# Query strips of the even layer, expert panels parted by contraction, and sample projections without a fold

## The chip, the cores and the metric

The kernel runs on one NeuronCore of one Trainium2 chip. The metric is the device time of one launch in microseconds (us), from the first to the last instruction and what lies around them. The core has five engines with instruction queues of their own: TensorE (PE; its weight loads are shown apart as PEld), VectorE (DVE), ScalarE (ACT), GpSimd (POOL) and SyncE (SP), which here only issues DMAs. They wait for each other by semaphores. PE's results go to PSUM, eight banks of 128 partitions by 512 fp32 numbers, and are copied or consumed from there by DVE and ACT. All weights stream from HBM through 16 DMA engines that the queues share.

## What is computed

One inference step of a two-layer decoder trunk on 256 prompt tokens (one sequence) and 32 sample tokens (8 sequences of 4), with a model width of 1024, all in fp32. Layer 0 ("even") is gated linear attention with 4 heads, in chunks of 16 tokens, beside a pooling mixer; layer 1 ("odd") is retention. Each is followed by a mixture of 64 experts with the 8 best per token and a shared expert, and then by a gate. Cut to what matters here:

```python
def step(S, inp):                       # even layer, one chunk of 16 (prompt) or 4 (sample) tokens
    qc, kc, vc, ac = inp
    b = jnp.cumsum(ac, axis=1)
    q_in = qc * jnp.exp(b)
    k_in = kc * jnp.exp(-b)
    o_inter = jnp.einsum('bchk,bhkv->bchv', q_in, S)      # queries times the carried state
    att = jnp.where(causal, jnp.einsum('bthk,bshk->bhts', q_in, k_in), 0.0)
    o_intra = jnp.einsum('bhts,bshv->bthv', att, vc)
    ...
    return S_new, o_inter + o_intra
...
mixed = jnp.concatenate([o_a, pooled], axis=-1)
return mixed @ w_out, ...                                  # out projection
...
x = layer_norm(ALPHA * x + h, ...)
h = jax.nn.silu(xt @ wg) * (xt @ wu)                       # one expert; its result is (h @ wd) * gate
x = layer_norm(ALPHA * x + f, ...)
gate = jax.nn.sigmoid(x @ w_ple_gate[i])                   # gates of each token
x = x + gate * (p[i] @ w_ple_proj[i])
```

## The kernel before

The order of the work is written out by hand, engine by engine; one function per engine and layer part, and semaphores between them. PSUM banks are dealt out by `plan_groups`, which walks the names of `group_order` and gives each the next bank in turn; PE's `begin(name)` waits until the bank's last user has freed it, and `end(...)` marks it full. `CH` names three chunks of tokens: 0 and 1 are the prompt's two halves of 128, 2 the 32 sample tokens.

**Queries times states (`even_pe`, L901 and L907).** The states that the 16 chunks carry lie in `SS` (head pair f, chunk i), those of the sample's 8 sequences in `gs0`. For each chunk but the first, the state (128 by 128) is the stationary operand and 32 query columns (two heads by 16 tokens) move; for each sequence 8 columns move. The results go straight into the banks `oT` (features by tokens) and `oTs`; behind them the pooling matrices follow (L912), then masked attention times values is added in the same banks (L919, L924). ACT squares and copies `oT`, PE sums the squares (L931), and the out projection follows (L1158, L1162, L1116).

**Sample rows of the out projection and of the gates (`tok`, L1105, and `fold`, L1124).** The contraction has 8 parts; part c goes with all 512 columns into the strip of 32 partitions number c % 4, so that four partial sums lie in four strips. ACT copies them to SBUF (`keep_strips`), and a matmul with a stacked identity adds them up (`fold`); DVE (`residual`, L2262) or ACT (`gate_half`) takes the sum of 32 rows. Each wide matrix has two column halves n, so this runs twice for the out projection of layer 0 and twice for the gates of each layer.

**Experts.** They go in pairs: `gate_up` (L1252), `turn_hidden` (L1259), `down` (L1266) and the sums of the pair before (L1228, L1224). A pair's weights are three panels of 2 MB in a ring of six slots: panel k = 0 and 1 each hold gate and up matrix of one expert of the pair, panel 2 both down matrices. `gate_up` waits for both of its panels before its first matmul. SP refills a slot when the bank that its panel's last matmul fills is marked; the first three pairs of loads stand before a loop, the rest in `two_pairs` (L768 to L781). One pair (`HOME`, the seventeenth in order) has its weights in SBUF outside the ring.

The names that the steps touch: `QI` (scaled queries), `QS` and `QSS` (new), `parts` and `Steps.empty`, which takes four strips with 128 columns each out of a bank, one instruction per strip.

Of the kernel before, what the change touches and what calls it, by code (L numbers as in the profile page):

```python
# [31 lines left out]
P = 128  # L32
# [14 lines left out]
H = 4  # L47
# [65 lines left out]
def constants():  # L113
# [17 lines left out]
            np.tile(inv.reshape(-1), (P, 1))]  # L131
# [50 lines left out]
def group_order():  # L182
# [6 lines left out]
    def out(tag, chunks=range(3)):  # L189
        g.extend((tag, j, n) for j in chunks for n in range(2))  # L190
        if 2 in chunks and tag[:2] in ("ou", "pg"):
            at = g.index((tag, 2, 1)) + 1
            g[at:at] = [(tag, "fold", n) for n in range(2)]

    for l in range(DEPTH):
        xt(f"xTa{l}", ORD[2:] if l else ORD)
        if l % 2 == 0:
# [59 lines left out]
        g.extend((f"pg{l}", "fold", n) for n in range(2))  # L257
        g.extend((f"pg{l}", 1, n) for n in range(2))
        if l + 1 < DEPTH:
# [56 lines left out]
def trunk(nc, A, O, C):  # L316
# [17 lines left out]
    with ExitStack() as ctx:  # L334
# [64 lines left out]
        invc = ce.take(64)  # L399

# [14 lines left out]
        QI = a.take(4 * T).rearrange("p (f k t) -> p f k t", f=2, k=2)  # L415
# [14 lines left out]
        AT = XTb[:, 4 * T:8 * T].rearrange("p (h t) -> p h t", h=4)  # L430

# [88 lines left out]

        def strip_sums(name):

            at = STATE if name[0] == "out0" else SIDE
            o = 0 if name[0] == "out0" else D
            return at[:, o + 512 * name[2]:o + 512 * name[2] + 512]
# [110 lines left out]
        def _(sp):  # L636
# [41 lines left out]
            for l in range(DEPTH):  # L678
# [57 lines left out]

                for pr in range(2):
                    for k in range(3):
# [25 lines left out]
                        expert_panel(n0 + 3 * pr + k, 2 * pr, k)  # L764
# [3 lines left out]
                def two_pairs(it, late):  # L768
                    for u in range(1 if isinstance(it, int) else 2):
# [7 lines left out]
                with sp.Fori(1, HOME // 2 + 1) as it:  # L777
# [3 lines left out]
                two_pairs(PAIRS // 2 - 1, 1)  # L781
# [27 lines left out]
        def even_pe(pe, st, begin, end, feat, tok):  # L809
# [75 lines left out]
            for h in range(H):  # L885
                ps = begin(("att", h))
                for j, (o, r) in enumerate(CH):
                    last = pe.matmul(ps[0:r, o:o + r], KI[:, h // 2, o:o + r], QI[:, h // 2, h % 2, o:o + r],
                                     start=True, stop=True)
                end(last, ("att", h))  # L890
# [5 lines left out]
            outs = []  # L896
# [6 lines left out]
            out4 = begin(("oTs",))[:, 0:H * TS].rearrange("p (h t) -> p h t", h=H)  # L903
            for f in range(2):
                for i in range(NSEQ):
                    c = DSEQ * i
                    pe.matmul(out4[:, 2 * f:2 * f + 2, c:c + DSEQ], gs0[:, f, i, :], QI[:, f, :, SEQ + c:SEQ + c + DSEQ],  # L907
                              start=(f == 0 and i == 0), stop=False, skip_group_check=True)
# [6 lines left out]
            for f in range(2):  # L915
                for k in range(2):
                    h = 2 * f + k
                    for j in range(2):
                        last = pe.matmul(outs[f][:, k, P * j:P * j + P], V[:, j, P * h:P * h + P],  # L919
                                         AT[:, h, P * j:P * j + P], start=False, stop=(k == 1 and j == 1),  # L920
                                         skip_group_check=True)
                end(last, ("oT", f))
            for h in range(H):
                last = pe.matmul(out4[:, h, :], V[0:TS, 2, P * h:P * h + P], AT[0:TS, h, SEQ:T],  # L924
                                 start=False, stop=(h == H - 1), skip_group_check=True)
# [7 lines left out]
        def odd_pe(pe, st, begin, end, feat, tok, fold, transpose_x):  # L933
# [122 lines left out]
        def _(pe):  # L1056
# [40 lines left out]
            def tok(name, lhs, rhs, r, n, w=512):  # L1097
# [3 lines left out]
                if r == TS and n >= 8 and name[0] not in ("v", "out1", "oute1"):  # L1101
# [17 lines left out]
            def fold(tag):  # L1119

                for n in range(2):
                    emptied(pe, (tag, 2, n))
                    ps = begin((tag, "fold", n))
                    end(pe.matmul(ps[0:TS, :], fold4, strip_sums((tag, 2, n)), start=True, stop=True), (tag, "fold", n))  # L1124

            pe.wait_ge(sem("ident_in"), 16)
            pe.wait_ge(sem("ones_set"), 1)
            for l in range(DEPTH):
# [9 lines left out]
                else:  # L1138
                    odd_pe(pe, st, begin, end, feat, tok, fold, transpose_x)
                if l % 2 == 0:  # L1140
# [23 lines left out]
                    fold(f"out{l}")  # L1164
# [90 lines left out]

                def turn_hidden(u, ps):
# [48 lines left out]
                def two_pairs(it, late=False):  # L1305

                    for u in range(2):
# [9 lines left out]
                        else:  # L1317
# [1201 lines left out]
```

## Time and profile before

| | |
|---|---|
| time, median of 3 runs (range) | 1671.39 us (1671.09 to 1671.58) |
| the profiled execution: its own time, its span | 1670.99 us, 1669.2 us |
| busy share of the span: PE, DVE, ACT, POOL | 95%, 32%, 20%, 9% |
| bytes from HBM, to HBM | 526.15 MB, 23.87 MB |
| mean granted TensorE clock | 0.983 |

The span runs from the first instruction to the last one; the rest of the execution's own time lies around it. The profile gives each instruction's start and length, what ended the idle time in front of it, and the TensorE clock that was granted (1.00 is 2.4 GHz, 0.50 is 1.2 GHz). In an instruction's line "ps<-arena 128*128 128x32" the first pair is the stationary operand, the second the result. Each fp32 matmul of the program stands as two instructions in the trace. The stages, in us from the span's start: the even layer to 172, routing to 210, experts of layer 0 to 699, gates to 748, the odd layer to about 1091, routing to 1129, experts of layer 1 to 1616, gates to the end.

### The profile page before, as it was taken

The page shows a single profiled execution, that of the slowest core. Times are in us where ns is not written, and L with a number is a line of the kernel's source. Part 1 is how long each engine was busy: PE and PEld are TensorE (multiplying, and loading weights), DVE is VectorE, ACT ScalarE, POOL GpSimd, SP SyncE. Part 2 cuts the span into 40 slices and gives each one's busy share as a digit, 9 for nine tenths or more (in the row PEclk, how much of TensorE's full clock was granted, in tenths as well). Part 3 has the DMA queues.
Part 4 walks back from the last instruction along what each step waited for, and adds up shares of the span by engine and source line. Part 5 has one row for each costly group of instructions (what it writes and reads, how often), then busy time and mean ns, then how long its engine had stood idle before and what let it go on. Part 6 is the DMA issues. An engine that isn't in the chain of part 4 may idle for free.

```text
span 1669.2 us, 21844 instructions
## 1 busy us (share of the span) xinstructions
PE 1587.6 (95%) x7954; PEld 799.2 (48%) x7954; DVE 539.7 (32%) x1322; ACT 341.4 (20%) x693; POOL 144.6 (9%) x221
## 2 busy tenths in 40 slices
PE   8999899999999999999999999989999999999998
PEld 5784544334344433446665755554443434443343
DVE  2145722222222222261434245372222222222225
ACT  2102122121122221231222222012212112221122
POOL 0330100000000000000011111010000000000000
PEclk9969999999999999999999999989999999999999
DMA  9623779999989999955385586577999998999970
GB/s 299 245 82 133 277 313 419 421 421 420 420 348 421 420 420 420 388 200 188 134 269 195 196 279 235 202 310 306 421 421 421 420 419 362 420 421 419 421 291 29
DMA packets 119271, 536.09 MB, mean 321 GB/s; under 512 B 17849, under 2 KB 29369, under 8 KB 69408
## 3 DMA queue, kind: packets, MB, share of 16 engines
q1 hardware_dynamic: 95975, 470.35, 70.5%
q0 software_dynamic: 21360, 61.64, 10.2%
q10 hardware_dynamic: 1872, 3.22, 0.6%
q8 instruction: 44, 0.72, 0.2%
q14 instruction: 20, 0.16, 0.0%
HBM read 526.15 MB, written 23.87 MB: 330 GB/s over the span
## 4 chain that ended last, share of the span: by engine, by line
PE 81%; DMA 11%; DVE 3%; issue 2%; ACT 1%; SPq 1%; POOL 0%; ACTq 0%; DVEq 0%
PE ps L1252 23%; PE ps L1116 12%; PE ps L1094 12%; DMA weights<-in_w_exp_up 11%; PE ps L1266 10%; PE ps L1228 5%; PE ps L1245 3%; PE ps L1224 2%; PE ps L1259 1%; PE ps L1010 1%; PE ps L1105 1%; PE ps L1286 1%; PE ps L988 1%; PE ps L901 1%; PE ps L1001 1%
## 5 line engine op out<-in xcount | busy, mean ns | idle before, releaser
L1252 PE MATMUL ps<-weights,x_feat 128*64 128x512 f32 x1984 | 437.8, 593 | 36.8 <-DMA weights<-in_w_exp_up 18.5
L1252 PEld LDWEIGHTS ps<-weights,x_feat 128*64 128x64 f32 x1984 | 147.1, 137 | 320.9 <-issue 318.2
L1266 PE MATMUL ps<-weights,arena 128*64 128x512 f32 x992 | 226.5, 598 | 0.9 <-ACT arena L1450 0.9
L1094 PE MATMUL ps<-x_feat,weights 128*128 128x288 f32 x832 | 210.2, 411 | 1.1 <-ACT x_feat L1450 1.1
L1094 PEld LDWEIGHTS ps<-x_feat,weights 128*128 128x128 f32 x832 | 159.9, 194 | 45.1 <-issue 3.8
L2104 DVE CAST split<-state 128x1024 fp32r<-128x1024 f32 (+1 forms) x66 | 44.7, 678 | 324.9 <-ACT state L1450 324.9
L2101 DVE SCALAR_TENSOR_TENSOR arena<-arena,ps 128x256 f32<-128x256 f32 x64 | 30.7, 480 | 365.3 <-ACT arena L1679 365.3
L2423 POOL DMA_INDIRECT arena<-x_rows,arena x64 | 63.6, 993 | 891.0 <-DVE arena L2094 845.9
L1450 ACT ACTIVATE state<-ps 128x512 f32<-128x512 f32 x132 | 78.8, 597 | 268.5 <-PE ps L1266 261.1
L1116 PE MATMUL ps<-weights,x_feat 128*128 128x512 f32 x288 | 126.7, 594 | 3.0 <-ACT x_feat L1476 3.0
L1266 PEld LDWEIGHTS ps<-weights,arena 128*64 128x64 f32 x992 | 65.7, 136 | 132.3 <-issue 130.9
L1679 ACT ACTIVATE arena<-ps 128x256 f32<-128x256 f32 x64 | 24.5, 383 | 444.6 <-PE ps L1252 444.6
L1228 PE MATMUL ps<-split,token_rows 128*128 128x512 f32 x256 | 111.8, 437 | 1.6 <-DVE y_low L2107 1.6
L1450 ACT ACTIVATE arena<-ps 128x256 f32<-128x256 f32 (+7 forms) x150 | 59.0, 405 | 222.4 <-PE ps L1116 84.5
L1228 PE MATMUL ps<-y_low,token_rows 128*128 128x512 f32 x256 | 100.8, 394 | 0.0
L1116 PEld LDWEIGHTS ps<-weights,x_feat 128*128 128x128 f32 x288 | 54.1, 190 | 69.8 <-issue 64.5
L1245 PEld LDWEIGHTS ps<-const,arena 128*128 128x128 f32 x512 | 62.3, 194 | 51.1 <-issue 51.1
L1116 PE MATMUL ps<-weights,arena 128*128 128x512 f32 x192 | 84.3, 592 | 0.0
L1450 ACT ACTIVATE x_feat<-ps 128x512 f32<-128x512 f32 x137 | 74.0, 588 | 49.8 <-PE ps L1245 45.9
L2107 DVE TENSOR_TENSOR y_low<-state,split 128x1024 fp32r<-128x1024 f32 (+1 forms) x66 | 78.7, 1193 | 2.3
L1245 PE MATMUL ps<-const,arena 128*128 128x128 f32 x512 | 74.4, 288 | 0.0
L1116 PEld LDWEIGHTS ps<-weights,arena 128*128 128x128 f32 x192 | 36.1, 190 | 41.6 <-issue 41.1
(289 smaller groups left out, 1280.8 us busy)
## 6 DMA issues: line engine op xcount, KB each, us to landing
weights<-in_w_exp_gate SPq DMA_DIRECT2D x124, 1024.0 KB, 14.8
weights<-in_w_exp_up SPq DMA_DIRECT2D x124, 1024.0 KB, 18.8
weights<-in_w_exp_down SPq DMA_DIRECT2D x124, 1024.0 KB, 16.9
weights<-in_w_in_c SPq DMA_DIRECT2D x24, 1024.0 KB, 8.1
arena<-in_state_ret POOLq DMA_DIRECT2D x20, 512.0 KB, 5.5
out_ret_sample<-arena POOLq DMA_DIRECT2D x20, 512.0 KB, 6.5
weights<-in_w_in_a SPq DMA_DIRECT2D x8, 1024.0 KB, 10.9
weights<-in_w_ple_gate SPq DMA_DIRECT2D x8, 1024.0 KB, 17.8
```

The costliest lines, as they stand in the source:

```text
L1094: last = pe.matmul(ps[:, 0:T], lhs(c), XT[:, c, :], start=(c == 0), stop=(c == n - 1))
L1116: last = pe.matmul(ps[0:r, 0:w], lhs(c), rhs(c), start=(c == 0), stop=(c == n - 1))
L1224: last = pe.matmul(PS[TS * q:TS * q + TS, 7, 0:256], TOK[u][:, SEQ:T].bitcast(F32), YF[:, 256 * q:256 * q + 256], start=False, stop=stop, ...
L1228: last = pe.matmul(bank((f"sum{l}", j, n)), TOK[u][:, P * j:P * j + P], y[:, 512 * n:512 * n + 512], start=False, stop=stop and y is YLO, ...
L1245: last = pe.transpose(ps[:, c * P:c * P + P], xc[:, 4 * q + c, :], ident)
L1252: last = pe.matmul(ps[64 * s:64 * s + 64, :], XGT[u][:, c, 64 * s:64 * s + 64], rhs, start=(c == 0), stop=(c == KC - 1))
L1266: last = pe.matmul(ps[64 * s:64 * s + 64, :], HT[u][:, c, 64 * s:64 * s + 64], wd[s][:, c, 512 * n:512 * n + 512], start=(c == 0), stop=(c ...
L1450: return act.activation(dst, src, ACT.Copy, **k)
L2101: return STT(HH[u], HS[u], META[u][:, 0:1], PS[:, 0, DE:2 * DE], ALU.mult, ALU.mult)
L2104: return dve.tensor_copy(YHI[:, c], YF[:, c])
L2107: return TT(YLO[:, c], YF[:, c], YHI[:, c].bitcast(F32), ALU.subtract)
L2423: pool.indirect_dma_start(XG[u], None, xd, bass.IndirectOffsetOnAxis(ap=GI[u], axis=0), bounds_check=last_row, oob_is_err=False).then_inc( ...
```

## The change

Three parts, in one change.

1. **Query strips.** The two operands change places: 32 query columns of a chunk are stationary, the state's 128 columns move, and the result (32 tokens-by-heads rows) goes to strip i % 4 of the new banks `qS` and `qSs`. `QI` gets a layout with those 32 columns side by side. For the sample, one stationary operand holds the queries of four sequences, so that a strip has rows of other sequences too. ACT copies the three banks to SBUF (`QS`; for `QSS` with a mask per partition, `own_strip`), and PE turns them with 8 matmuls against the identity and 4 against the stacked one, adding them to `oT` and `oTs`. The first chunk takes part now, with a state that POOL sets to zero. The pooling matmuls stand before the new banks' use.
2. **Panels parted by contraction.** For the first and the last pair of each layer's ring, panel 0 holds parts 0 to 3 of the contraction of all four gate and up matrices, and panel 1 parts 4 to 7. `gate_up_halves` waits for each panel apart. After the first half of the very first pair it raises `half_consumed`, and SP refills that panel's slot upon it instead of upon the end of the whole gate-and-up. SP's second pair of pairs is written out ahead of its loop.
3. **No fold.** The sample rows of the out projection (layer 0) and of the gates (both layers) run with the branch that was there for other products: each strip takes 128 of the 512 columns over the whole contraction, 32 matmuls instead of 8. `fold` and `keep_strips` are gone, and the reader takes four pieces of 32 by 128.

```diff
@@ group_order
+            g.extend((("qS", 0), ("qS", 1), ("qSs",)))
+            g.extend(("pool", f) for f in range(4))
             g.extend((("oT", 0), ("oT", 1), ("oTs",)))
-            g.extend(("pool", f) for f in range(4))
...
@@ trunk
+        QS = [STATE[:, 512 * f:512 * f + 512] for f in range(2)]
+        QSS = keys[:, 0:512]
...
@@ SP
+                def contraction_panel(num, e0, k):
+
+                    s = slot_full[num % SLOTS]
+                    dst = wp(num).rearrange("p (s m x) -> p s m x", s=2, m=2)
+                    for m, w in enumerate((A["w_exp_gate"], A["w_exp_up"])):
+                        src = w[l, e0:e0 + 2].rearrange("e (p c) n -> p e (c n)", c=KC)
+                        sp.dma_start(dst[:, :, m, :], src[:, :, 1024 * k:1024 * k + 1024]).then_inc(s, 16)
...
+                            elif isinstance(it, int) and it == 1 and u + k == 0:
+                                sp.wait_ge(sem("half_consumed"), l + 1)
                             else:
                                 sp.wait_ge(bank_full[0], base[0] + 2 * (u + late) - 3 + 4 * it)
-                            expert_panel(n0 + 3 * u + k, 4 * it + 2 * u, k)
...
@@ even_pe
             for f in range(2):
-                out2 = begin(("oT", f)).rearrange("p (k t) -> p k t", k=2)
-                outs.append(out2)
-                for i in range(1, NCA):
-                    pe.matmul(out2[:, :, CA * i:CA * i + CA], SS[:, f, i, :], QI[:, f, :, CA * i:CA * i + CA],
-                              start=(i == 1), stop=False, skip_group_check=True)
...
+                ps = begin(("qS", f))
+                for i in range(NCA):
+                    q, g = i % 4, i // 4
+                    last = pe.matmul(ps[TS * q:TS * q + TS, P * g:P * g + P], QI[:, f, i].rearrange("p k c -> p (k c)"), SS[:, f, i, :],
+                                     start=(g == 0), stop=(g == 3), skip_group_check=True)
+                end(last, ("qS", f))
...
+                emptied(pe, ("qS", f))
+                for g in range(4):
+                    tokens_of = out2[:, :, 64 * g:64 * g + 64].rearrange("p k (i c) -> p i k c", c=CA)
+                    last = pe.matmul(tokens_of, QS[f][:, P * g:P * g + P], ident, start=False, stop=(g == 3),
+                                     skip_group_check=True)
...
+            emptied(pe, ("qSs",))
+            for f in range(2):
+                for g in range(2):
+                    last = pe.matmul(out4[:, 2 * f:2 * f + 2, CA * g:CA * g + CA], QSS[:, P * (2 * f + g):P * (2 * f + g) + P],
+                                     fold_all[:, 0:TS], start=False, stop=(f == 1 and g == 1), skip_group_check=True)
...
@@ tok
-                if r == TS and n >= 8 and name[0] not in ("v", "out1", "oute1"):
+                if name[0] == "vstrips":
...
@@ PE, experts
+                def gate_up_halves(u, ring, it, ps):
+                    for k in range(2):
+                        n = ring + k
+                        pe.wait_ge(slot_full[n % SLOTS], 32 * (n // SLOTS + 1) + 32 * it)
+                        w = wp(n).rearrange("p (s m c n) -> p s m c n", s=2, m=2, c=4)
+                        for c in range(4):
+                            for s in range(2):
+                                last = pe.matmul(ps[64 * s:64 * s + 64, :], XGT[u][:, 4 * k + c, 64 * s:64 * s + 64],
+                                                 w[:, s, :, c, :], start=(k == 0 and c == 0), stop=(k == 1 and c == 3))
+                        if it == 0 and k == 0:
+                            last.then_inc(sem("half_consumed"), 1)
+                    return last
...
@@ ACT, even layer
+                    for f in range(2):
+                        full(act, ("qS", f))
+                        st.free(copy(QS[f], bank(("qS", f))), ("qS", f))
+                    full(act, ("qSs",))
+                    act.wait_ge(sem("even_table"), 16)
+                    st.free(copy(QSS, bank(("qSs",)), scale=own_strip), ("qSs",))
...
@@ DVE residual
-                name, r = (f"out{l}", "fold" if j == 2 else j, n), CH[j][1]
+                name, r = (f"out{l}", j, n), CH[j][1]
...
-                st.free(STT(x, x, ALPHA, bank(name)[0:r, :], ALU.mult, ALU.add), name)
+                st.empty(name, r, lambda ps, c: STT(x[:, c], x[:, c], ALPHA, ps[0:r, :], ALU.mult, ALU.add))
```

PE's order in the even layer from the last state updates on, as it was; `ps` is PSUM, `arena` the region that holds states, queries and values, `ln_rows` holds `gs0`, and an `x` behind a shape counts matmuls (not trace instructions).

```order
L855 MATMUL ps<-arena,side 64x128 x32
L901 MATMUL ps<-arena 128x2x16 x30
L907 MATMUL ps<-arena,ln_rows 128x2x4 x16
L912 MATMUL ps<-arena 128x288 x4
L919 MATMUL ps<-x_feat,arena 128x128 x8
L924 MATMUL ps<-x_feat,arena 128x32 x4
L931 MATMUL ps<-x_feat,small 128x512 x2
```

The same place now; the lines are those of the changed kernel, `state` is `QS`, and L938 and L948 are the matmuls against the identities.

```order
L866 MATMUL ps<-arena,side 64x128 x32
L912 MATMUL ps<-arena 32x128 x32
L919 MATMUL ps<-ln_rows,arena 32x128 x16
L925 MATMUL ps<-arena 128x288 x4
L933 MATMUL ps<-x_feat,arena 128x128 x4
L938 MATMUL ps<-const,state 128x4x2x16 x4
L933 MATMUL ps<-x_feat,arena 128x128 x4
L938 MATMUL ps<-const,state 128x4x2x16 x4
L943 MATMUL ps<-x_feat,arena 128x32 x4
L948 MATMUL ps<-const,arena 128x2x16 x4
L955 MATMUL ps<-x_feat,small 128x512 x2
```

The 46 products of 128 rows have become 48 of 32 rows, and 12 matmuls have come in between attention and the squares.

SP's queue where the ring's first refill is issued, before (gate and up matrices of the second expert and both down matrices follow in the same way).

```order
L766 TENSOR_LOAD small [waits flag_ready]
L766 ISA x2
L777 UNCONDITIONAL_BRANCH
L777 ISA
L734 ISA [waits bank_full_0]
L734 DMA weights<-in_w_exp_gate 128x2048
L734 DMA weights<-in_w_exp_up 128x2048
```

And now.

```order
L771 TENSOR_LOAD small [waits flag_ready]
L771 ISA x2
L728 DMA weights<-in_w_exp_gate 128x2048 [waits half_consumed]
L728 DMA weights<-in_w_exp_up 128x2048
L728 DMA weights<-in_w_exp_gate 128x2048 [waits bank_full_0]
L728 DMA weights<-in_w_exp_up 128x2048
L728 DMA weights<-in_w_exp_down 128x2048 [waits bank_full_1]
```

Nothing has moved past anything there; the first refill stands ahead of the loop now and waits for another semaphore.

DVE's order around the sample rows of layer 0's out projection, before.

```order
L2276 TENSOR_SCALAR x_tok<-x_tok,small 128x1024
L2294 TENSOR_SCALAR x_feat<-ps,small 128x128 x4
L2262 SCALAR_TENSOR_TENSOR x_tok<-x_tok,ps 32x512 x2
L2269 BN_STATS small<-x_tok 32x6 x2
L2271 BN_AGGR small<-small 32x2
```

And now.

```order
L2312 TENSOR_SCALAR x_tok<-x_tok,small 128x1024
L2330 TENSOR_SCALAR x_feat<-ps,small 128x128 x4
L2298 SCALAR_TENSOR_TENSOR x_tok<-x_tok,ps 32x128 x8
L2305 BN_STATS small<-x_tok 32x6 x2
L2307 BN_AGGR small<-small 32x2
```

Two instructions of 512 columns have become eight of 128, in the same place.

## Rows read from the trace of the kernel before

**Rows 1.** Waits of PE over the whole span: us in total, times, longest us.

```profile
PE ps L1252 <- DMA weights<-in_w_exp_up: 18.5, 16, 1.6
PE ps L1252 <- issue: 16.0, 12, 1.6
```

**Rows 2.** Timeline of PE, even layer's end: start, us, instruction, idle before it.

```profile
97.43 6.33 PE L855 MATMUL ps<-arena,side 32*64 32x128 f32 x64 [2.97 <-DVE side L1806]
103.69 13.01 PE L901 MATMUL ps<-arena 128*128 128x32 f32 x60
116.51 6.97 PE L907 MATMUL ps<-arena,ln_rows 128*128 128x8 f32 x32
123.33 4.19 PE L912 MATMUL ps<-arena 128*128 128x288 f32 x8
127.31 2.75 PE L919 MATMUL ps<-x_feat,arena 128*128 128x128 f32 x16
130.00 1.07 PE L924 MATMUL ps<-x_feat,arena 32*128 32x32 f32 x8
```

**Rows 3.** Windows of PE there: us, busy (instructions), granted clock, DMA share, GB/s.

```profile
94.00:97.00 3.00, 0.46 (x5) 1.00 0.22 67
99.00:128.00 29.00, 29.00 (x150) 0.50 0.18 41
129.00:131.00 2.00, 2.00 (x18) 1.00 0.00 0
```

**Rows 4.** Timeline of ACT, even layer's end.

```profile
129.21 0.60 ACT L1541 ACTIVATE x_feat<-ps 128x512 f32<-128x512 f32 x1 [41.37 <-PE ps L919]
```

**Rows 5.** Timeline, other places: 288 columns at full clock; 32-row products, layer 1.

```profile
79.47 7.93 PE L1094 MATMUL ps<-x_feat,weights 128*128 128x288 f32 x32
...
1028.33 1.96 PE L1111 MATMUL ps<-weights,arena 128*32 128x128 f32 x64
...
1030.35 1.22 DVE L1971 SCALAR_TENSOR_TENSOR x_tok<-x_tok,ps 32x128 f32<-32x128 f32 x4 [1.23 <-PE ps L1111]
```

**Rows 6.** Windows in layer 0's expert stage, columns as in rows 3.

```profile
210.00:217.00 7.00, 6.95 (x32) 1.00 0.01 2
217.00:219.00 2.00, 1.53 (x13) 1.00 0.60 66
...
320.00:440.00 120.00, 109.40 (x573) 1.00 1.01 420
460.00:480.00 20.00, 20.00 (x110) 1.00 0.68 273
```

**Rows 7.** Timeline of SP's queue, layer 0: first refills of the ring.

```profile
217.32 0.35 SPq L734 DMA_DIRECT2D weights<-in_w_exp_gate  x1
...
230.71 0.33 SPq L734 DMA_DIRECT2D weights<-in_w_exp_gate  x1
```

**Rows 8.** Timeline of PE: first and last pair's gate-and-up, layers 0 and 1.

```profile
210.05 7.09 PE L1252 MATMUL ps<-weights,x_feat 128*64 128x512 f32 x32 [1.13 <-ACT x_feat L1450]
681.64 7.09 PE L1252 MATMUL ps<-weights,x_feat 128*64 128x512 f32 x32 [1.62 <-issue]
1598.93 7.09 PE L1252 MATMUL ps<-weights,x_feat 128*64 128x512 f32 x32 [1.49 <-issue]
```

**Rows 9.** Timeline, layer 0's out projection: sample rows, copies, fold, residual.

```profile
161.49 3.64 PE L1105 MATMUL ps<-weights,arena 128*32 128x512 f32 x32
164.26 1.36 DVE L2294 TENSOR_SCALAR x_feat<-ps,small 128x128 f32<-128x128 f32 x4
166.31 0.68 DVE L2262 SCALAR_TENSOR_TENSOR x_tok<-x_tok,ps 32x512 f32<-32x512 f32 x1 [0.69 <-PE ps L1124]
```

**Rows 10.** Timeline, layer 0's gates: fold, last feature turn, last logits.

```profile
729.33 1.90 PE L1124 MATMUL ps<-side,const 128*32 128x512 f32 x4
729.44 1.36 DVE L2294 TENSOR_SCALAR x_feat<-ps,small 128x128 f32<-128x128 f32 x4 [7.50 <-PE ps L1082]
731.17 14.00 PE L1116 MATMUL ps<-weights,x_feat 128*128 128x512 f32 x32
```

More of the change, by code:

```diff
@@ L399, in trunk @@
         invc = ce.take(64)
+        own_strip = ce.take(1)
         gate_ops = a.take(8 * RANK + 256 + T)
@@ L763, in _, with two_pairs @@
                         wait_slot(n0 + 3 * pr + k)
-                        expert_panel(n0 + 3 * pr + k, 2 * pr, k)
+                        if pr == 0 and k < 2:
+                            contraction_panel(k + n0, 0, k)
+                        else:
+                            expert_panel(n0 + 3 * pr + k, 2 * pr, k)
                 sp.wait_ge(sem("flag_ready"), l + 1)
                 go = sp.value_load(flagi[0:1, 0:1], min_val=0, max_val=1)
-                def two_pairs(it, late):
-                    for u in range(1 if isinstance(it, int) else 2):
+                def two_pairs(it, late, pairs=2):
+                    for u in range(pairs):
                         for k in range(3):
@@ L887, in even_pe @@
                 for j, (o, r) in enumerate(CH):
-                    last = pe.matmul(ps[0:r, o:o + r], KI[:, h // 2, o:o + r], QI[:, h // 2, h % 2, o:o + r],
-                                     start=True, stop=True)
+                    last = pe.matmul(ps[0:r, o:o + r], KI[:, h // 2, o:o + r],
+                                     QI[:, h // 2, o // CA:(o + r) // CA, h % 2, :], start=True, stop=True)
                 end(last, ("att", h))
@@ L915, in even_pe @@
             for f in range(2):
+                out2 = begin(("oT", f)).rearrange("p (k t) -> p k t", k=2)
                 for k in range(2):
@@ L931, in even_pe, with odd_pe @@
                 end(pe.matmul(ps, onesA, SQE[:, :, o:o + r], start=True, stop=True), ("ms", j))
-        def odd_pe(pe, st, begin, end, feat, tok, fold, transpose_x):
+        def odd_pe(pe, st, begin, end, feat, tok, transpose_x):
             for kind, h, i in odd_schedule():
@@ L1117, in tok @@
                 end(last, name)
[L1119 to L1124, printed above, removed]
             pe.wait_ge(sem("ident_in"), 16)
@@ L1138, in _ @@
                 else:
-                    odd_pe(pe, st, begin, end, feat, tok, fold, transpose_x)
+                    odd_pe(pe, st, begin, end, feat, tok, transpose_x)
                 if l % 2 == 0:
@@ L1316, in two_pairs @@
                             pe.wait_ge(sem("home_in"), 96 * (l + 1))
-                        else:
+                        elif not (first or last):
                             for n in range(ring, ring + 2):
@@ L1320, in two_pairs @@
                         pe.wait_ge(bank_free[0], base[0] + uses(0, pr, 0))
-                        gate_up(u, HOME_UP if home else [wp(ring), wp(ring + 1)], PS[:, 0, :]).then_inc(bank_full[0], 1)
+                        if first or last:
+                            gate_up_halves(u, ring, it, PS[:, 0, :]).then_inc(bank_full[0], 1)
+                        else:
+                            gate_up(u, HOME_UP if home else [wp(ring), wp(ring + 1)], PS[:, 0, :]).then_inc(bank_full[0], 1)
                         pe.wait_ge(bank_free[1], base[1] + uses(1, pr, 0))
@@ L1462, in norm_root @@
                 st.tell(act.activation(rstd[:, j:j + 1], bnag[:, 2 * j + 1:2 * j + 2], ACT.Sqrt, bias=eps), sem("std", l, k))
-            def keep_strips(tag):
-                for n in range(2):
-                    full(act, (tag, 2, n))
-                    st.free(copy(strip_sums((tag, 2, n)), bank((tag, 2, n))), (tag, 2, n))
             def x_affine(tag, l, k, chunks):
@@ L1723, in gate_half @@
                     r = CH[j][1]
-                    name = (f"pg{l}", "fold" if j == 2 else j, n)
+                    name = (f"pg{l}", j, n)
                     full(act, name)
@@ L1727, in gate_half @@
                         act.wait_ge(sem("gated", l), 2 * i + n - 1)
-                    st.free(act.activation(SG[n][0:r, :], bank(name)[0:r, :], ACT.Sigmoid), name)
+                    st.empty(name, r, lambda ps, c: act.activation(SG[n][0:r, c], ps[0:r, :], ACT.Sigmoid))
                 def gate(i):
@@ L1792, in even_dve @@
                         dve.wait_ge(sem("queries_zeroed"), 1)
-                    st.run(STT(QI[0:64, f, 0, :], ps[0:64], DKA ** -0.5, EB[0:64, f, :], ALU.mult, ALU.mult))
-                    st.free(STT(QI[64:128, f, 1, :], ps[64:128], DKA ** -0.5, EB[64:128, f, :], ALU.mult, ALU.mult), ("qk", f))
+                    for k in range(2):
+                        rows = slice(64 * k, 64 * k + 64)
+                        ins = STT(QI[rows, f, :, k, :], ps[rows].rearrange("p (i c) -> p i c", c=CA), DKA ** -0.5,
+                                  EB[rows, f, :].rearrange("p (i c) -> p i c", c=CA), ALU.mult, ALU.mult)
+                        if k:
+                            st.free(ins, ("qk", f))
+                        else:
+                            st.run(ins)
                 else:
@@ L2225, in gate @@
                 for n in range(2):
-                    emptied(dve, (f"pg{l}", "fold" if j == 2 else j, n))
+                    emptied(dve, (f"pg{l}", j, n))
                     cols = slice(512 * n, 512 * n + 512)
@@ L2328, in even_pool @@
             store(O["pool_sample"][0, :, 0:PBUF - DSEQ, :], A["state_pool"][0, :, DSEQ:PBUF, :], s)
+            st.run(pool.memset(SS[:, :, 0, :], 0.0))
+            st.after
             st.tell(pool.memset(QI, 0.0), sem("queries_zeroed"))
```

46 lines of the change are left out of this document (20 added, 26 removed), and 2 rows, old and new, of the table FIXED_BANKS.

## The prediction

> **What bounds the kernel now.** TensorE. I read the page first for its busy shares (PE 95% by the table above), then the list of PE's waits. Only one kind of wait comes back often: L1252, the gate-and-up of an expert pair, for its weights, 28 times with 34.5 us in all [rows 1]. That is the most that earlier loads can give. The second kind of loss is not idle time: in the windows [rows 3] PE is busy for the whole of 99 to 128 us, but at half the clock (0.50, which is 1.2 of 2.4 GHz). So in two places of the program two different things are to be counted: durations at the granted clock where PE is full, and arrival times where it waits for DMA.
>
> **Even layer's end, what goes.** PE waits 2.97 us for DVE at 94.46, does the state updates L855, and from 103.69 on runs without a gap to 131.07 [rows 2]. The parts: L901 13.01 us for 60 instructions and L907 6.97 for 32 (both 0.217 each, though one moves 32 columns and the other 8), L912 4.19 for 8, L919 2.75 for 16, L924 1.07 for 8. The whole is 131.07 - 103.69 = 27.38 us. All stands before the squares, the out projection and the routing, which follow from its end, so that each us saved here is one of the total, if nothing else becomes late. What could: ACT had been idle for 41.37 us at that point [rows 4], so the three new copies (0.60 us each by the same row's form) find it free and lie behind PE's pooling products.
>
> **What comes.** 48 strip products are 96 instructions. Layer 1 has products of the same shape, 128 by 32 stationary, 128 columns moving, four strips in turn: L1111, 64 in 1.96 us, 0.0306 each at full clock [rows 5]. At half clock I double that: 0.061, 5.9 us for 96. The other bound is L855, in place and at half clock, 6.33/64 = 0.099 each [rows 2], 9.5 us; but it has two strips of 64 columns instead of four of 32, so I take L1111's price. The pooling L925 costs 2.0 us at full clock (L1094, also 288 columns, 7.93/32 = 0.248 each [rows 5]) and 4.2 at half. Then come 16 instructions of attention times values, 16 turns, 8 of the sample and 8 more turns: 48. L924 at full clock has 1.07/8 = 0.134 each, and I take it for all: 6.4 us at full clock.
>
> So the clock decides. In [rows 2, 3] it is at 1.00 up to 97, at 0.50 from 99 to 128, and at 1.00 again from 129; the products with 288 columns had begun at 123.33, 5.6 us before, and before them narrow ones had run for 20 us without raising it. The strips move 128 columns, four of them side by side. I take it that the clock rises 5.6 us after the first of them: 5.9 + 2.0 + 6.4 = 14.3 us, **13.1 us gained**. If only the pooling products raise it, they take 4.2, and 1.4 us more at 0.268 do 5 of the 48; the rest is 43 x 0.134 = 5.8. The sum is then 5.9 + 4.2 + 1.4 + 5.8 = 17.3, 10.1 gained. A clock that never falls would take at most 3 us off the strips: 16 gained.
>
> Here a rule stands against the size of this gain. The Trainium skill, "TensorE: Matmul & The Clock Gate", section "LDWEIGHTS (loading the stationary operand)", gives the time of a weight load as its columns over 1.2, in ns, whatever the rows: 107 ns for 128 columns, 27 for 32. If loads set the pace at that price, 92 x 0.107 = 9.8 us would go and 96 x 0.027 + 24 x 0.107 = 5.2 come, an estimate of 4.6 us from that page. The trace disagrees on the size here: 0.217 per instruction at granted clock 0.50 [rows 2, 3].
>
> **First pair of a layer.** All loads of the ring's first six slots are done before its first matmul: the DMA share is 0.01 in 210 to 217 [rows 6], which is the first gate-and-up, 7.09 us from 210.05 [rows 8]. The first refill goes out at 217.32 [rows 7], in the two us behind it hardly anything moves (66 GB/s), and later the engines are full: 420 GB/s in 320 to 440, where PE is busy for 109.40 of 120 us [rows 6]. There DMA sets the pace, so bytes that flow earlier come off PE's waits. `half_consumed` comes after half of the 7.09 us, at about 213.85 by count of instructions: 217.32 - 213.85 = 3.44 us earlier. Panel 0 alone is freed then; panel 1 still waits for 217.3, but 2.1 MB at 420 GB/s keep the engines in work for 5.0 us, longer than the 3.44. The next place where the queue could run dry is the refill issued at 230.71 [rows 7]: three panels of 2.1 MB and 0.5 MB gathered take 16.2 us at that rate, from 215.9 (213.85 and the two us behind an issue) to 232.1, while what is issued at 230.71 flows by 232.7. Up to 0.6 us are lost there. I take **3.1 us**, between 2.8 and 3.44. It is kept: after the home pair the share falls to 0.68 for 20 us [rows 6], since the ring is full, so that DMA then follows PE. Layer 1 runs the same instructions: 3.1 again.
>
> **Last pair.** PE waits 1.62 us at 681.64 and 1.49 at 1598.93 for panel 1 [rows 8]. Panel 0 lands one panel, 5.0 us, earlier; its half takes 3.5 us of PE, more than the wait, so both waits go: **3.1 us**. The down panel follows panel 1 by 5.0 us, to some 686.6. PE asks for it once gate-and-up is through, 681.64 - 1.62 + 7.09 = 687.1, and hidden rows are turned; the slack is small, and a loss of up to 1 us stays in the range.
>
> **No fold.** In layer 0 the last in the chain is DVE: L2294 at 164.26 until 165.62, then the residual, 0.68 per half [rows 9], begun at 166.31 after the fold. Four pieces of 32 by 128 take 1.22 in L1971 [rows 5], so eight 2.44 instead of 1.36, but they begin when L2294 ends: 165.62 + 2.44 = 168.1. The two halves of now end at 166.31 + 1.36 = 167.7 at the earliest, later if the fold's second half keeps the second one waiting. So 0 to 0.4 are lost; I take **0.2 us**. PE's strips stay about as they are (3.64 now [rows 9], 128 x 0.0306 = 3.9 by L1111). At the gates the fold of 1.90 us ends at 731.2, when L1116 begins, but the last feature turn of that chunk ends on DVE at 729.44 + 1.36 = 730.80 [rows 10]: that is what L1116 then waits for, and 0.4 us gained pays the strips' 0.2 to 0.3. I count nothing for both layers, plus or minus 0.5.
>
> **Sum.** 13.1 + 6.2 + 3.1 - 0.2 = 22.2 us off the profiled execution's 1671.0 gives 1648.8. That execution lies 0.4 under the median of the three runs, so I say **1649 us**.
>
> **The rivals.** No change can be told from none within 0.2%, 3.3 us, and a mechanism on the far side has to eat 22 us first.
> - *The clock rises only with the pooling* (0.16): 3.0 us less, 1651.8. For it: 20 us of busy PE with narrow products did not raise it, and neither did L855 with its 128 columns.
> - *Strips at L855's price and a late clock* (0.10): 3.6 us more on top, 1655.4. For it: the same place and clock. Against: the strips of L1111.
> - *The refill's gain is swallowed* (0.12): if panels of 4 KB rows load slower, or the queue runs dry at 230.71 for longer, the 6.2 us are lost: 1655.0. Against: the full engines in [rows 6].
> - *The last pair's wait moves to its second half or to the down panel* (0.04): 1652.
> - *The turns give it back* (0.02): stationary operands of 128 columns set the pace to the end of the stage, at L901's 0.217 for each of the 48: 5.9 + 4.2 + 10.4 = 20.5, 6.9 gained, 1655.2. Against: L924, whose operand has 128 columns too, took 0.134. By the page cited above, with its 4.6 us, it would be 1657.3.
> - *Slower* (0.03): the clock stays at 0.50 behind the strips, through squares and out projection to 165.1. The 34 us of PE work there then take 68, 1649 + 34 = 1683. It decides when half clock lasts about 22 us longer than to 131. For it: PE has a new place to wait, for ACT's copies before the turns. Against: 4 us of pooling and attention products stand in between, and copies of 0.60 us are done by then.
> - *More* (0.02): the clock doesn't fall, 1646.
>
> The forecast has 0.51 and its own range, 1647 to 1650.5. The cases of 1651.8 to 1655.4 belong in the range, and below it the bounds of the refill and of the clock: 1645 to 1656. Faster by over 0.2%: all but the slower case and what I can't name, 0.95; same 0.02; slower 0.03.
>
> **What would show it.** The strips L912 and L919 together at 5.9 us or 9.5; the granted clock at 1.00 from about 109 or from about 115; `oTs` done at about 118 instead of 131. ACT's copies without a wait of PE at L938. SP's first refill 3.4 us after gate-and-up begins, and waits of L1268 in layer 0 some 3 us less before the home pair; no wait ahead of the last gate-and-up, and none inside it. Eight residuals of 0.31 in layer 0; L1140 following DVE's last turn in the gates. The forecast is wrong if DMA turns out to have had slack elsewhere, or if the stage from 103.7 on is not followed by what depends on it alone.

## The result, and the profile after

The changed kernel takes 1653.49 us (median of 4 runs, 1651.97 to 1655.55) against 1671.24 before: a ratio of 0.9895, 95% interval 0.9878 to 0.9912, so 17.7 us less where 22.2 were forecast. The profiled execution took 1652.17 us with a span of 1650.4, 18.8 less than before's.

What answers to [rows 2]: PE's timeline at the even layer's end, after.

```profile
96.97 6.50 PE L866 MATMUL ps<-arena,side 32*64 32x128 f32 x64 [2.98 <-DVE side L1842]
103.41 3.64 PE L912 MATMUL ps<-arena 128*32 128x128 f32 x64
106.82 1.56 PE L919 MATMUL ps<-ln_rows,arena 128*32 128x128 f32 x32
108.32 2.21 PE L925 MATMUL ps<-arena 128*128 128x288 f32 x8
110.36 1.05 PE L933 MATMUL ps<-x_feat,arena 128*128 128x128 f32 x8
111.25 1.06 PE L938 MATMUL ps<-const,state 128*128 128x128 f32 x8
...
115.03 1.08 PE L948 MATMUL ps<-const,arena 128*128 128x32 f32 x8
115.94 2.18 PE L955 MATMUL ps<-x_feat,small 128*128 128x512 f32 x6
```

In a MATMUL line the second pair is the moving operand, partitions by columns, and not the result: a strip `128*32 128x128` moves 128 columns and yields 32 rows. From the first strip to the squares it is 115.94 - 103.41 = 12.53 us, where it was 131.00 - 103.69 = 27.31. No wait stands ahead of L938, so ACT's copies are hidden. The windows of PE there (columns as in [rows 3]):

```profile
106.00:107.00 1.00, 1.00 (x24) 0.50 0.00 0
107.00:108.00 1.00, 1.00 (x29) 0.56 0.00 0
108.00:109.00 1.00, 1.00 (x19) 1.00 0.02 8
```

The clock is back at some 107.9, 4.5 us after the first strip and before any pooling product has begun. In [rows 3] it was at 0.50 until 128.

SP's first refills, which answer to [rows 7], and the windows of the expert stages, which answer to [rows 6]:

```profile
199.02 0.33 SPq L728 DMA_DIRECT2D weights<-in_w_exp_gate  x1
...
202.45 0.33 SPq L728 DMA_DIRECT2D weights<-in_w_exp_gate  x1
...
215.84 0.33 SPq L728 DMA_DIRECT2D weights<-in_w_exp_gate  x1
```

```profile
209.00:215.00 6.00, 6.00 (x30) 1.00 1.03 427
215.00:221.00 6.00, 6.00 (x39) 1.00 0.88 328
221.00:227.00 6.00, 6.00 (x30) 1.00 1.02 422
...
1131.00:1137.00 6.00, 6.00 (x39) 1.00 0.89 299
```

The first refill goes out 3.43 us ahead of the second. But behind the issue at 215.84, the one that [rows 7] has at 230.71, the rate dips to 328 GB/s, in layer 1 to 299: at 422 GB/s, six such us lack 6 x 94 / 422 = 1.3 and 6 x 123 / 422 = 1.7 us of transfer.

PE's waits, to be held against [rows 1], and PE's timeline at the last pairs' first products and at the end of layer 1's experts (the first line stands at the edge of a shorter stretch and counts 10 of the 32 instructions):

```profile
PE ps L1268 <- DMA weights<-in_w_exp_up: 14.6, 13, 1.6
PE ps L1268 <- issue: 13.0, 10, 1.6
...
PE ps L1140 <- issue: 2.7, 1, 2.7
```

```profile
662.24 2.31 PE L1279 MATMUL ps<-weights,x_feat 128*64 128x512 f32 x10
...
1577.35 7.04 PE L1279 MATMUL ps<-weights,x_feat 128*64 128x512 f32 x32
...
1594.57 0.40 PE L1244 MATMUL ps<-y_low,token_rows 128*128 128x512 f32 x1
1597.71 7.13 PE L1140 MATMUL ps<-weights,arena 128*128 128x512 f32 x16 [2.75 <-issue]
```

The waits for weights are 27.6 us instead of 34.5, and neither last pair (L1279) waits. New is 2.75 us ahead of layer 1's first projection. Held against before, the same places of PE's program come earlier by:

| place | us earlier |
|---|---|
| first gate-and-up, layer 0 | 14.71 |
| home pair, layer 0 | 17.93 |
| last pair, layer 0 | 19.40 |
| last logits, layer 0 | 19.62 |
| first gate-and-up, layer 1 | 18.36 |
| home pair, layer 1 | 20.32 |
| last pair, layer 1 | 21.58 |
| first projection behind it, and the end | 18.71, 18.80 |

Up to layer 1's last pair the kernel is 21.6 us ahead, near the forecast of 22.2. It gives back 1.3 us between the layers and 2.9 at that projection.

### The profile page after: what moved, and what is told of

It is laid out like the page before. It is cut to its first block, busy times and chain, and to the rows that moved or that the text cites. A ratio compares the mean times of both kernels' runs of the same rounds, so it can differ in the third digit from the quotient of the medians.

```text
span 1650.4 us, 22440 instructions
## 1 busy us (share of the span) xinstructions
PE 1568.3 (95%) x8258; PEld 791.6 (48%) x8258; DVE 540.2 (33%) x1328; ACT 342.1 (21%) x702; POOL 144.8 (9%) x222
## 3 DMA queue, kind: packets, MB, share of 16 engines
q10 hardware_dynamic: 1872, 3.22, 0.6%
## 4 chain that ended last, share of the span: by engine, by line
PE 83%; DMA 10%; DVE 3%; issue 2%; ACT 1%; SPq 1%; POOL 0%; ACTq 0%; DVEq 0%
PE ps L1268 22%; PE ps L1140 13%; PE ps L1118 12%; PE ps L1295 11%; DMA weights<-in_w_exp_up 10%; PE ps L1244 6%; PE ps L1261 3%; PE ps L1240 2%; PE ps L1279 2%; PE ps L1288 1%; PE ps L1135 1%; PE ps L1034 1%; PE ps L1315 1%; PE ps L1012 1%; PE ps L1025 1%
## 5 line engine op out<-in xcount | busy, mean ns | idle before, releaser
L1268 PE MATMUL ps<-weights,x_feat 128*64 128x512 f32 x1856 | 409.3, 593 | 27.7 <-DMA weights<-in_w_exp_up 14.6
L1268 PEld LDWEIGHTS ps<-weights,x_feat 128*64 128x64 f32 x1856 | 136.6, 137 | 294.7 <-issue 294.7
L1118 PE MATMUL ps<-x_feat,weights 128*128 128x288 f32 x832 | 210.6, 411 | 1.1 <-issue 1.1
L1118 PEld LDWEIGHTS ps<-x_feat,weights 128*128 128x128 f32 x832 | 160.2, 194 | 45.5 <-issue 4.0
## 6 DMA issues: line engine op xcount, KB each, us to landing
weights<-in_w_exp_gate SPq DMA_DIRECT2D x124, 1024.0 KB, 14.7
```

Of the source, the lines that this page charges most:

```text
L1118: last = pe.matmul(ps[:, 0:T], lhs(c), XT[:, c, :], start=(c == 0), stop=(c == n - 1))
L1268: last = pe.matmul(ps[64 * s:64 * s + 64, :], XGT[u][:, c, 64 * s:64 * s + 64], rhs, start=(c == 0), stop=(c == KC - 1))
```

## The experiments

My first theory: the strips' gain is whole, the last refill's dip costs 3 us, half clock at the end of layer 0's gates comes of leaving out the fold, and PE waits at the projection for a block of its own code. The rival: loads set the time in the end, so that PE runs into them at the projection and gives back what it has gained.

**Each part alone.** The kernel before with one part of the change, `e1_strips`, `e2_panels`, `e3_nofold`. Of the diff above, the first takes these lines and what belongs to them:

```diff
+                ps = begin(("qS", f))
...
+                    last = pe.matmul(tokens_of, QS[f][:, P * g:P * g + P], ident, start=False, stop=(g == 3),
```

the second these:

```diff
+                        if first or last:
+                            gate_up_halves(u, ring, it, PS[:, 0, :]).then_inc(bank_full[0], 1)
...
+                                sp.wait_ge(sem("half_consumed"), l + 1)
```

and the third these:

```diff
-                if r == TS and n >= 8 and name[0] not in ("v", "out1", "oute1"):
+                if name[0] == "vstrips":
...
-                fold(f"pg{l}")
```

> The kernel before with the query strips alone. Theory: the stage from the first query product to the sample's output shrinks by 14.8 us (27.4 to 12.6), the clock is back at full speed some 4.5 us after the first strip, and all of it reaches the end, about 1656.3 us. Rival (the gain at the end of layer 0's gates and at the ends of the expert stages is eaten by loads that don't come earlier): 1658 to 1660 us.

Measured: 1666.23 us, ratio 0.9971 (0.9962 to 0.9981). Neither theory nor rival. The stage takes 12.91 us, nearly as short as in the whole change, and PE is 14.78 us ahead at layer 0's first gate-and-up, 15.25 at the last pair. Then this, in PE's timeline:

```profile
683.65 0.40 PE L1245 MATMUL ps<-y_low,token_rows 128*128 128x512 f32 x1
688.90 9.00 PE L1133 MATMUL ps<-weights,arena 128*128 128x512 f32 x16 [4.85 <-issue]
```

The same kind of wait, in layer 0 this time, and behind it the projection at half clock, 9.00 us instead of 7.03. PE is only 8.24 us ahead after it.

> The kernel before with the panels parted by contraction alone. Theory: 3.2 and 2.0 us from the early refill in layers 0 and 1, 1.4 and 1.2 us from the last pairs, together 7.8 us: 1663.4 us, and no wait of PE ahead of layer 1's first projection. Rival (that projection's wait of 2.75 us comes from this part, because PE has run up to loads that are still under way): 1666.1 us, with the wait in the trace.

Measured: 1664.01 us, ratio 0.9960 (0.9947 to 0.9974), 7.2 us less; no wait ahead of the projection in either layer. The early refills gave 3.4 and 1.4 us up to the home pairs, the last pairs 1.0 and 1.4. So the loads that this part moves don't bring a wait at the projection by themselves.

> The kernel before without the folds alone. Theory: 0.25 us lost in layer 0's out projection, 0.2 and 0.1 us gained at the last logits of the two layers, and 1.3 us lost to half clock where layer 0's gates end, since PE's 1.4 us wait there is in one piece now: about 1672.4 us. Rival (nothing but the sums that the prediction has): 1671.2 to 1671.5 us and half clock for 3.4 us there as before.

Measured: 1671.01 us, ratio 1.0005 (0.9996 to 1.0014): nothing, as the rival said. Half clock at the end of layer 0's gates lasts no longer than before here, though PE waits there 1.35 us in one piece. That part of my theory fell: the clock is at 0.50 there for 3.4 us before and here, for 6.8 us in the changed kernel's profile and in the strips kernel's, which has the folds, and not at all in the panels kernel's. The changed kernel's repeat below has 3.4 us. So it goes with the run, not with the fold.

The three parts alone take off 5.0, 7.2 and 0.2 us, 12.4 in all, where the whole change takes off 17.7: the strips alone lose 7.0 us at that projection.

**Empty instructions ahead.**

```diff
+            for _ in range(128):
+                pe.nop()
             pe.wait_ge(sem("ident_in"), 16)
```

> The changed kernel with 128 empty instructions ahead of TensorE's first one, 8 KB of code, half a block of its instruction queue. Theory (PE waits 2.75 us ahead of layer 1's projection for a block of its own code): the wait goes or moves to another place, and the runs of 1652 and 1655 us change their shares; 1649.4 us where it goes. Rival (PE waits there for the projection's weights or for a semaphore): the wait stays at 2.75 us and the time at 1652 to 1655 us.

Measured: 1652.51 us, ratio 0.9892 (0.9876 to 0.9907), the wait 2.41 us. The blocks of the instruction queue were fetched at the same places of the program as without padding, and neither trace lists an empty instruction, so this run shifted no code that can be seen and tells nothing of where it lies. It is the changed kernel once more. The projection behind the wait ran at half clock in it (8.59 us), so that such a wait can cost 1.6 us more than its length.

**The second pair in halves as well.**

```diff
-                        if pr == 0 and k < 2:
-                            contraction_panel(k + n0, 0, k)
+                        if k < 2:
+                            contraction_panel(n0 + 3 * pr + k, 2 * pr, k)
...
-                            elif isinstance(it, int) and it == 1 and u + k == 0:
-                                sp.wait_ge(sem("half_consumed"), l + 1)
+                            elif isinstance(it, int) and it == 1 and k == 0:
+                                sp.wait_ge(sem("half_consumed"), 2 * l + u + 1)
...
-                        if first or last:
+                        if halved or last:
```

> The changed kernel with the second pair of each layer parted by contraction as well and the refill of its first panel's slot issued after half of its gate-and-up. Theory (the transfer queue runs dry for 1.3 us in layer 0 and 1.7 us in layer 1 ahead of that refill: 328 and 299 GB/s over six us where 422 is the rate): the gaps go, 3.0 us less than the changed kernel, about 1650.5 us, and the early refill's gain up to the home pair rises to 4.5 us in layer 0 and 3.7 in layer 1. Rival (the dip comes from the rows of 4 KB or from the gathers, not from a late issue): the dip stays, within 0.5 us of the changed kernel.

Measured: 1651.99 us, ratio 0.9889 (0.9872 to 0.9906). Its windows, to be held against the dip above:

```profile
215.00:221.00 6.00, 6.00 (x39) 1.00 1.01 422
...
1131.00:1137.00 6.00, 6.00 (x41) 1.00 1.01 418
```

The dip is gone in both layers, and PE gains 4.33 and 2.99 us up to the home pairs instead of 3.22 and 1.96. The mechanism is shown; its worth is 1.1 and 1.0 us there, less than the 3.0 that I expected. The times of the two kernels, 1.5 us apart, don't tell them apart yet.

**Without the branch that is jumped over.** Behind the last pair PE has a branch for experts with too many tokens. The inputs never take it; PE jumps over its code. This kernel leaves out that part of the computation, the branch, on PE alone.

```diff
-                with pe.If(go > 0):
-                    with pe.Fori(0, 4) as m:
...
-                    pe.wait_ge(sem("ov_summed", l), 4 * PAIRS)
                 pe.nop()
```

> The changed kernel without TensorE's branch for experts with too many tokens, which is jumped over for these inputs; the other engines keep theirs. Theory (behind the jump PE waits for a 16 KB block of its own code, which lands 2.4 us before PE goes on): no jump, no wait ahead of layer 1's first projection, 2.75 us less, about 1650.7 us. Rival (a semaphore or the projection's weights hold it): the wait stays, 1653 us.

Measured: 1648.75 us, ratio 0.9860 (0.9844 to 0.9877), 4.7 us less than the changed kernel. PE's timeline at the projection:

```profile
1597.08 0.40 PE L1244 MATMUL ps<-y_low,token_rows 128*128 128x512 f32 x1
1597.31 7.03 PE L1140 MATMUL ps<-weights,arena 128*128 128x512 f32 x16
```

No wait, with the same semaphores and loads around it. The wait was 2.75 us; from the first strip to the end the two profiled runs differ by 3.3 us (1543.7 and 1547.0), and the rest of the 4.7 lies within the spread of some 4 us between runs. Two more runs make this firm: the strips alone without the branch, and the kernel before without it.

> The kernel before with the query strips alone and without TensorE's branch for experts with too many tokens (never taken here). Theory (the strips' 14.8 us are whole, and the lone strips kernel lost 8 to 9 of them to the wait for code at layer 0's projection, to half clock behind it and behind layer 0's gates): the wait of 4.85 us is gone, 1657 to 1659 us. Rival (the gain of the strips is eaten in the expert stages or by loads that set the time in the end): 1663 to 1666 us as with the branch.

Measured: 1658.77 us, ratio 0.9929 (0.9916 to 0.9942): 7.5 us less than the strips with the branch, and no wait in layer 0's projection.

> The kernel before without that branch: the control for the two kernels without it. Its trace shows no wait ahead of either projection, so nothing should change: 1671 us, within 1 us. If it gains 4 us or more, leaving out the branch does more than take away a wait for code, and the reading of the other two falls.

Measured: 1670.32 us, ratio 0.9996 (0.9988 to 1.0005). Without a wait to take away, leaving out the branch changes nothing that can be told from the runs' spread.

**Clock or operands?** The kernel before with the pooling matmuls moved ahead.

```diff
+            for g in range(4):
+                pe.wait_ge(sem("pool_d"), g + 1)
+                ps = begin(("pool", g))
+                end(pe.matmul(ps[:, 0:T], wpool[:, P * g:P * g + P], DD[:, g, :], start=True, stop=True), ("pool", g))
             outs = []
```

> The kernel before with the pooling matmuls of 288 columns moved ahead of the queries-times-states products, nothing else. It tells the clock from the operands. If the clock rises upon the pooling and stays, its 4.2 us are followed by 92 products at 0.11 to 0.13 us instead of 0.217 and 24 at 0.134: 17.5 to 19.7 us instead of 27.4, 8 to 10 us gained at the sample's output, 1661.5 to 1663.5 us if nothing is lost behind it. If narrow moving operands bring the clock down again, the products take 0.217 as before and at most 2 us are gained: then the strips' gain is theirs and not the clock's alone.

Measured: 1671.45 us, ratio 0.9998 (0.9985 to 1.0011). PE's timeline, and its windows:

```profile
103.77 4.21 PE L899 MATMUL ps<-arena 128*128 128x288 f32 x8
107.77 9.74 PE L905 MATMUL ps<-arena 128*128 128x32 f32 x60
117.31 6.97 PE L911 MATMUL ps<-arena,ln_rows 128*128 128x8 f32 x32
124.14 3.76 PE L919 MATMUL ps<-x_feat,arena 128*128 128x128 f32 x16
```

```profile
108.00:109.00 1.00, 1.00 (x8) 0.63 0.00 0
109.00:112.00 3.00, 3.00 (x29) 1.00 0.54 97
112.00:113.00 1.00, 1.00 (x7) 0.58 0.75 184
113.00:119.00 6.00, 6.00 (x30) 0.50 0.42 117
```

The clock rises at 108.7, 5.0 us after the first pooling product, and falls again at 112.2 while PE is busy without a gap with products of 32 moving columns. So pooling brings the clock up in this place as the strips do, but this order of the work is worth nothing: the narrow products behind it run at half clock again, and they, not the order, are what the strips replace.

**The last pair as before.**

```diff
-                            if isinstance(it, int) and it > 1 and k < 2:
-                                contraction_panel(n0 + 6 * it + k, 4 * it, k)
-                            else:
-                                expert_panel(n0 + 3 * u + k, 4 * it + 2 * u, k)
+                            expert_panel(n0 + 3 * u + k, 4 * it + 2 * u, k)
...
-                        if first or last:
+                        if first:
```

> The changed kernel with the last pair of each layer loaded and waited for as before. Theory: the waits ahead of the last gate-and-up are back with 1.4 to 1.6 us each, 2.9 us more, about 1656.4 us; if PE waits ahead of layer 1's projection for loads or code that come at a fixed time, that wait shrinks by the same and only layer 0's share is seen, 1655.0 us.

Measured: 1655.47 us, ratio 0.9909 (0.9892 to 0.9925), 2.0 more than the changed kernel, with overlapping ranges. The waits are back, and the one at the projection has shrunk from 2.75 to 1.42:

```profile
1578.08 7.09 PE L1265 MATMUL ps<-weights,x_feat 128*64 128x512 f32 x32 [1.45 <-issue]
...
1597.13 3.27 PE L1137 MATMUL ps<-weights,arena 128*128 128x512 f32 x7 [1.42 <-issue]
```

So by these two profiles most of what the last pair gains in layer 1 was waited away behind the jump: its wait of 1.45 us is back, and 1.33 are gone from the other.

**The second pair in halves with padding**, 64 and 192 empty instructions.

> The changed kernel with the second pair in halves too, and 64 empty instructions ahead of TensorE's first (4 KB, a quarter of a block). Where the target of the jump falls into a block that PE has at hand, the wait ahead of the projection goes in both layers: about 1649 us. Where it doesn't, a wait of 2.2 to 4.9 us stands in one of the layers as before, 1651 to 1654 us. If the place of the code played no part the wait of 2.18 us would stay as it was with no padding.

Measured: 1649.82 us, ratio 0.9871 (0.9857 to 0.9885).

> The same with 192 empty instructions (three quarters of a block). Expected as for 64: 1649 us where no wait stands ahead of either projection, 1651 to 1654 us with one. Of the two paddings and none, the one without a wait is the version to keep.

Measured: 1649.72 us, ratio 0.9875 (0.9861 to 0.9889). Both still wait at layer 1's projection, 2.71 and 2.23 us; the padding has moved no code here either. They count as repeats of the second pair in halves: its 12 runs have a median of 1650.6 us, the 8 of the changed kernel (with and without padding) one of 1653.0. That is 2.4 us, though the two ranges overlap; the 1.1 and 1.0 us in the traces are the firmer figure. It is the fastest full version of this study.

## Why the prediction was right, and where it was short

The time lies in the stated range, 4.5 us above the forecast. Almost all of that, 1.3 and 2.9 us, is lost between the layers and at layer 1's projection. That PE was so near the forecast up to there is in part luck: the strips gave 1.7 us more than their term, the pairs 1.4 less than theirs.

- **Even layer's end:** forecast 13.1, measured 27.31 - 12.53 = 14.8. The clock rose while the strips ran, as the likeliest case had it, and 4.5 us after the first instead of 5.6 (2.6 to 5.3 in the other profiles with strips). L912's 0.057 and L919's 0.049 per instruction stand for 0.061, and what comes behind the pooling took 5.6 us for 6.4. By places the 14.8 are 14.7 from the replaced products (19.64 us, now 4.91) and 1.9 from pooling at full clock, less 1.9 for the longer tail. The profile's weight loads (PEld) show the same: at half clock those of 128 columns took 333 ns each, one and a half at a time, those of the strips 172 ns, three at a time. The case that only pooling raises the clock, and that of L855's price (0.099), are out. The 4.6 us that were worked out there from the figure of the Trainium skill, "TensorE: Matmul & The Clock Gate", section "LDWEIGHTS (loading the stationary operand)", are less than a third of what came: the strips' 0.05 us at half clock stand against 0.217, and what follows them runs at full clock.
- **First pair:** 3.1 forecast for each layer, 3.2 and 2.0 measured. One step that was short is "up to 0.6 us are lost there": the queue ran dry for 1.3 and 1.7 us ahead of the refill that 230.71 had stood for, and the kernel with the second pair in halves closed that gap. The other is "Layer 1 runs the same instructions: 3.1 again": between the first gate-and-up and the home pair PE waited 10.6 us for weights in layer 0 before, but only 9.2 in layer 1, and now waits 7.8 and 7.7. Layer 1 had 1.4 us less to give.
- **Last pair:** both waits went, as forecast, and neither half nor down panel waits. Up to its start it is 1.5 and 1.3 us net, together 2.7 for 3.1: the rest of the way from the home pair took some 0.2 us longer in each layer.
- **No fold:** 0.2 lost at layer 0's out projection (L1106's third group comes 14.81 us earlier, the squares 15.06), 0.2 and 0.1 gained at the last logits; alone, nothing. Right.
- **What the sum did not have:** PE's wait behind the jump, 2.75 us in the profiled run, and the 1.3 us between the layers, where the clock was at 0.50 behind the gates for 6.8 us instead of 3.4, which the repeat with padding doesn't show. Without the jump the time is 1648.75, and 1649 was forecast; so close a match rests on misses that cancel. The sum went by what each part removes and adds at its own place; that a new wait can arise 1,500 us behind an edit was in no rival.

Why the wait stands in layer 1 in the changed kernel, in layer 0 in the one with strips alone, and nowhere in four others that have the jump (before, panels alone, no fold alone, pooling ahead), was not settled: it was to be tried by shifting the code, and the padding shifted none. Left open too is the spread of some 4 us between runs of one kernel, as wide as several of the terms here. One part of it is seen at the start: in the profiled run without the branch the first 64 products of L1118 took 17.74 us, in the changed kernel's 16.68.

## What to carry to other kernels

It can pay to lay small products out with the short side stationary and the long one moving, in strips side by side: here they were about as many as before, ran at 0.05 us instead of 0.217 at the same half clock, and the clock came back while they ran. Which of the three does it (fewer stationary columns, more moving ones, four strips at once) was not tried apart. A load that is released earlier helps in full only until the next one that isn't; follow the queue to the place where it runs dry again. And after a change of TensorE's program look at what stands behind its jumps, far from the edit too: one wait there took a third of what the strips gave when they were alone, and half clock behind it 2 us more.

## What the hardware showed that I had not expected

The clock fell while PE was busy the whole time: in the kernel with pooling ahead it went from 1.00 to 0.50 at 112.2 us under products of 32 moving columns, and stayed there until 132.6.

PE waited behind its jump in seven of the eleven profiled kernels that have it, 1.4 to 4.9 us in one of the two layers, and in none of the three without it. In the changed kernel PE's last product before the jump ends at 1594.97. The transfers of the next window, 1595 to 1596, have one packet of an instruction queue:

```profile
q1 hardware_dynamic: 101, 0.20, 55.7%
q8 instruction: 1, 0.02, 6.9%
```

By narrower windows it starts between 1595.2 and 1595.4, and it takes 1.1 us (6.9% of 16 engines' 1 us); PE goes on at 1597.71. In all seven waits such a packet starts 2.2 to 2.7 us before PE goes on, however long PE has stood: at 686.2 in the strips alone, where PE goes on at 688.90 after 4.85 us, and at 1594.9 with the last pair as before, where it goes on at 1597.13 after 1.42. A packet by itself is no sign of a wait: with no fold alone one starts at 1617.7, and PE goes on at 1618.33 without one. The Trainium skill, "Runtime: NRT & Kernel Launch", section "Instruction fetch mechanics", says that a taken branch whose target lies outside the blocks at hand must wait for it to be fetched by DMA. The traces agree, by the packets above and by the two kernels that lost the wait with the jump; that the block fetched is the one the jump leads to is argued from this, not shown.
